# Turning the cached latents of one more sequence by on-chip transfers and VectorE instead of TensorE

## The reference

```
q_lat  = einsum('bqhd,chd->bqhc', q_nope, w_uk)            # 8 samples, 8 heads, 128 latents
s_past = einsum('bqhc,bkc->bhqk', q_lat, lat_past) + einsum('bqhr,bkr->bhqk', q_rope, kr_past)
p      = softmax(concat(s_past, s_new) * MLA_SCALE)
ctx    = einsum('bhqk,bkc->bqhc', p_past, lat_past) + p_new * c_kv
```

## Time and profile before

| | us |
|---|---|
| median of 3 runs | 1266.18 |
| lowest, highest | 1266.0, 1266.7 |
| the profiled execution | 1266.02 |
| its span, first to last instruction | 1264.2 |
| TensorE busy in it | 1250.9 (99%) |
| VectorE busy | 549.7 (43%) |
| ScalarE busy | 250.5 (20%) |

### The profile page before, as it was taken

One profiled execution on the slowest core, in us unless ns is written; L12 is line 12 of the kernel. 1 busy time (PEld: TensorE's weight loads), 2 busy tenths in 40 slices (PEclk: granted clock), 3 DMA queues, 4 the chain that ended last, 5 costly groups with the idle time before them and its releaser, 6 DMA issues.

```text
span 1264.2 us, 18049 instructions
## 1 busy us (share of the span) xinstructions
PE 1250.9 (99%) x7142; PEld 1022.8 (81%) x7142; DVE 549.7 (43%) x1387; ACT 250.5 (20%) x640; POOL 153.0 (12%) x210
## 2 busy tenths in 40 slices
PE   8999999999999999999999999999999999999997
PEld 6878777776888888888888787777778888888886
DVE  7866646323235333321178746463241453324212
ACT  3432414311100111110033324243111011111000
POOL 2012442010000000020001134511000000000000
PEclk9999999999999999999999999999999999999999
DMA  9433576357454444464454344755564544444440
GB/s 342 155 100 101 134 254 227 130 188 170 122 152 148 147 143 147 148 225 150 148 154 142 100 115 150 249 205 177 140 173 126 149 143 149 150 150 150 151 138 35
DMA packets 93971, 198.49 MB, mean 157 GB/s; under 512 B 41680, under 2 KB 42736, under 8 KB 91072
## 3 DMA queue, kind: packets, MB, share of 16 engines
q1 hardware_dynamic: 84624, 156.15, 40.4%
q0 software_dynamic: 8768, 40.84, 9.4%
q10 hardware_dynamic: 496, 0.36, 0.1%
HBM read 183.86 MB, written 9.25 MB: 153 GB/s over the span
## 4 chain that ended last, share of the span: by engine, by line
PE 95%; DVE 4%; ACT 1%; issue 0%; DMA 0%; SPq 0%; DVEq 0%; ACTq 0%
PE banks L573 77%; PE banks L1063 2%; PE banks L1076 1%; PE banks L1111 1%; PE banks L1074 1%; PE banks L968 1%; PE banks L717 1%; DVE arena L1715 1%; PE banks L996 1%; PE banks L675 0%; PE banks L1012 0%; DMA arena<-in_x 0%; DVE arena L2114 0%; PE banks L873 0%; PE banks L590 0%
## 5 line engine op out<-in xcount | busy, mean ns | idle before, releaser
L573 PE MATMUL banks<-arena 128*128 128x264 f32 x4512 | 1032.3, 388 | 5.7 <-DVE arena L1609 4.9
L573 PEld LDWEIGHTS banks<-arena 128*128 128x128 f32 x4512 | 851.0, 190 | 169.2 <-issue 13.2
L1217 ACT ACTIVATE arena<-banks 128x256 f32<-128x256 f32 (+8 forms) x252 | 92.6, 391 | 403.7 <-PE banks L573 293.2
L2217 DVE TENSOR_SCALAR arena<-arena 128x256 f32<-128x256 f32 x44 | 18.2, 414 | 130.2 <-ACT arena L1217 130.0
L2250 DVE SCALAR_TENSOR_TENSOR arena<-banks,arena 128x264 f32<-128x264 f32 x16 | 6.9, 433 | 134.2 <-PE banks L573 134.2
L2431 POOL COPY arena<-arena 128x2 f32<-128x2 f32 x44 | 13.7, 310 | 377.6 <-ACT arena L1217 275.9
L1248 ACT ACTIVATE arena<-banks 128x264 f32<-128x264 f32 x32 | 12.6, 392 | 130.6 <-PE banks L573 130.6
L2110 DVE COPY arena<-banks 128x512 f32<-128x512 f32 x24 | 16.6, 690 | 36.7 <-PE banks L1063 36.5
L1529 ACT ACTIVATE arena<-arena 128x256 f32<-128x256 f32 x44 | 18.4, 417 | 66.3 <-DVE arena L2219 66.3
L2224 DVE SCALAR_TENSOR_TENSOR arena<-arena 128x256 f32<-128x256 f32 x44 | 18.7, 426 | 26.6 <-ACT arena L1529 26.6
L2229 DVE TENSOR_TENSOR arena<-arena,banks 128x256 f32<-128x256 f32 x42 | 17.7, 422 | 26.4 <-PE banks L573 26.3
(11 more groups left out here) (447 smaller groups left out, 1072.5 us busy)
## 6 DMA issues: line engine op xcount, KB each, us to landing
arena<-in_weights SPq DMA_DIRECT2D x229, 512.0 KB, 3.6
arena<-in_weights SPq DMA_DIRECT2D x113, 256.0 KB, 3.5
arena<-in_s POOLq DMA_DIRECT2D x2, 2048.0 KB, 10.9
out_ss_o<-arena POOLq DMA_DIRECT2D x16, 256.0 KB, 3.1
arena<-in_mla_w POOLq DMA_DIRECT2D x4, 1024.0 KB, 6.7
arena<-arena SPq DMA_DIRECT2D x64, 64.0 KB, 2.4
arena<-in_c POOLq DMA_DIRECT2D x4, 512.0 KB, 6.3
out_sc_o<-arena POOLq DMA_DIRECT2D x16, 128.0 KB, 3.8
```

The costliest lines, as they stand in the source:

```text
L573: mm = nc.tensor.matmul(dst, ring[:, at_:at_ + 128], rhs[:, j, :], start=(start and j == 0), stop=(stop and j == k - 1))
L1217: return A(dst, src, ACT.Copy, scale=scale)
L2217: link(ts(cv, fc[:, j % 3, 0:TP], w[0], par[:, Q_FB + j:Q_FB + j + 1], ALU.mult, ALU.add))
```

## The change

Sequence 5 joins 6 and 7. Its blocks are laid out by 16 on-chip transfers, whose source is `lat[5]` and whose target is `ltt[:, 1]` itself, once the scores of sequence 3, the last reader of that half of `ltt`, are done. VectorE then turns them in place in `ltt[:, 1]`. TensorE no longer transposes sequence 5, and ScalarE and VectorE no longer copy its four banks. SyncE has the transfers ahead of unit 54 (sequence 5), 56 and 57 (sequences 6 and 7 as before).

VectorE's order: `turn(5)` comes right behind `pages(4)`, ahead of the three pieces that stood around `pages(5)`. The four pieces between sequences 5 and 6 become five, on all engines.

```diff
+IN_BLOCKS = 5, 6, 7
@@ schedule()
+    def mark(*sequences):
+        at_ = (34 + piece[0]) // 2 + SLOTS - 1
+        for n in sequences:
+            while at_ in marks:
+                at_ += 1
+            marks[at_] = n
     for n in range(4):
         pages(n)
+    mark(5)
     add("ss"); half(1); add("mxT", 1, "V"); ...
-    pages(4); half(2); pages(5); half(4); pages(6); pages(7); add("ss", 1, "A", 1)
+    pages(4); half(2); pages(5); half(5); pages(6); pages(7); add("ss", 1, "A", 1)
@@ build()
+        def blocks(n):
+            return lat[n - 6] if n >= 6 else ltt[:, n % 2].rearrange("p i n -> p (i n)")
@@ SyncE, blocks_of_latents
-                sp.wait_ge(*out(l, "cx", 0))
+                ...
+                elif n == 5:
+                    sp.wait_ge(*out(l, "ss", 0))
+                else:
+                    sp.wait_ge(*out(l, "cx", 0))
                 sp.wait_ge(*at(l, f"lat_in{n}", 32))
@@ TensorE, pages
-                    if n < 6:
+                    if n not in IN_BLOCKS:
                         for i in range(4):
                             b = claim("ltr", 4 * n + i)
...
-                        pe.wait_ge(*at(l, "lat_turned", 4 * (n - 5)))
+                        pe.wait_ge(*at(l, "lat_turned", 4 * (IN_BLOCKS.index(n) + 1)))
@@ TensorE
                 pages(5)
-                half(4)
+                half(5)
                 pages(6)
@@ ScalarE
                 pages(5)
-                half(6)
+                half(7)
@@ VectorE
+                def turn(n):
+                    dve.wait_ge(*at(l, f"lat_in{n}", 32))
+                    if n >= 2:
+                        dve.wait_ge(*scored(n - 2))
+                    V.transpose(krt[:, n % 2, :], key[n]).then_inc(*up("key_turned"))
+                    dve.wait_ge(*at(l, f"lat_blocks{n}", 256))
+                    for i in range(4):
+                        V.transpose(ltt[:, n % 2, i, :], blocks(n)[:, 512 * i:512 * i + 512]).then_inc(*up("lat_turned"))
                 pages(4)
-                half(2)
-                pages(5)
-                half(4)
-                pages(6)
-                pages(7)
+                turn(5)
+                half(3)
+                half(5)
+                turn(6)
+                half(1)
+                turn(7)
+                half(1)
                 top(1, 2)
```

More of the change, by code:

```diff
@@ L98, in schedule @@
 def schedule():
-    s, piece = [], [0]
+    s, piece, marks = [], [0], {}
+    def mark(*sequences):
[4 more added lines that the diff above has]
+            marks[at_] = n
     def add(name, n=1, reader="A", first=0):
@@ L149, in schedule @@
         pages(n)
+    mark(5)
     add("ss"); half(1); add("mxT", 1, "V"); half(1); add("mxB", 1, "V"); half(3); add("lsum", 1, "V"); add("cx")
-    at_context = (34 + piece[0]) // 2
+    mark(6, 7)
     half(2); add("cmb", 1, "V")
-    pages(4); half(2); pages(5); half(4); pages(6); pages(7); add("ss", 1, "A", 1)
+    pages(4); half(2); pages(5); half(5); pages(6); pages(7); add("ss", 1, "A", 1)
     half(2); add("mxT", 1, "V", 1); half(1); add("mxB", 1, "V", 1); half(4); add("lsum", 1, "V", 1); add("cx", 1, "A", 1); half(3); add("cmb", 1, "V", 1); half(len(PIECES) - piece[0])
@@ L160, in schedule @@
     add("fd", 8, "V")
-    return s, at_context + SLOTS - 1
+    return s, marks
 SCHED, BLOCKS_AT = schedule()
@@ L201 @@
     decay_masked=1, diag_set=3, ffn_conv=22, ffn_sconv=2, ffn_stanh=2, ffn_tail=22, ffn_tanh=22, ffn_zeros=1, fh_loaded=16,
-    hidden=2, hidden_norm=16, norm_raw=16, norm_square=16, norm_sum=14, hist_loaded=16, key_copied=2, key_turned=8, lat_turned=8, **{f"lat_blocks{n}": 256 for n in (6, 7)}, **{f"lat_in{n}": 32 for n in range(8)},
+    hidden=2, hidden_norm=16, norm_raw=16, norm_square=16, norm_sum=14, hist_loaded=16, key_copied=2, key_turned=8, lat_turned=12, **{f"lat_blocks{n}": 256 for n in IN_BLOCKS}, **{f"lat_in{n}": 32 for n in range(8)},
     inverse=1, inverse_turned=1, m_loaded=64, mdecay_exp=1, mdecay_in=4, mdecay_masked=1, merged=8, mla_q=16, mla_kv=16,
@@ L458, in build @@
         last_rms = bank("fd", 1)[:, 0:TT]
+        def blocks(n):
+            return lat[n - 6] if n >= 6 else ltt[:, n % 2].rearrange("p i n -> p (i n)")
         def quarter_of_latents(n, b, q):
-            return (lat[n - 6][32 * q:32 * q + 32, 512 * b:512 * b + 512].rearrange("i (r j) -> i r j", r=NR),
+            return (blocks(n)[32 * q:32 * q + 32, 512 * b:512 * b + 512].rearrange("i (r j) -> i r j", r=NR),
                     lat[n][32 * b:32 * b + 32, :].rearrange("i (r q j) -> i r q j", r=NR, q=4)[:, :, q, :])
@@ L499, in blocks_of_latents @@
             def blocks_of_latents(l, n):
-                sp.wait_ge(*out(l, "cx", 0))
+                if n == 0:
+                    sp.wait_ge(*out(l, "uq", 7))
+                elif n == 4:
+                    sp.wait_ge(*at(l, "page_scored", 3))
+                elif n == 5:
+                    sp.wait_ge(*out(l, "ss", 0))
+                else:
+                    sp.wait_ge(*out(l, "cx", 0))
                 sp.wait_ge(*at(l, f"lat_in{n}", 32))
@@ L512, in _ @@
                     sp.wait_ge(w_started, u - SLOTS + 2)
-                if u % UNITS in (BLOCKS_AT, BLOCKS_AT + 1):
-                    blocks_of_latents(u // UNITS, 6 + u % UNITS - BLOCKS_AT)
+                if u % UNITS in BLOCKS_AT:
+                    blocks_of_latents(u // UNITS, BLOCKS_AT[u % UNITS])
                 for h, at_, n in runs[u]:
@@ L1070, in pages @@
                     else:
-                        pe.wait_ge(*at(l, "lat_turned", 4 * (n - 5)))
+                        pe.wait_ge(*at(l, "lat_turned", 4 * (IN_BLOCKS.index(n) + 1)))
                     for i in range(4):
-                        turned = heads(ltt[:, n % 2, i, :], 32) if n >= 6 else turned_lat(n)[:, :, 32 * i:32 * i + 32]
+                        turned = heads(ltt[:, n % 2, i, :], 32) if n in IN_BLOCKS else turned_lat(n)[:, :, 32 * i:32 * i + 32]
                         nc.tensor.matmul(heads(sb[32 * i:32 * i + 32, :], 32), ql_pad[:, g, s_, :], turned,
@@ L1471, in pages @@
                 def pages(n):
-                    for i in (0, 2):
+                    for i in () if n in IN_BLOCKS else (0, 2):
                         act.wait_ge(*out(l, "ltr", 4 * n + i))
@@ L2050, in _, with scored @@
                 last.then_inc(*up("query_blocks"))
+                def scored(n):
+                    if n % 4 == 3:
+                        return out(l, "ss", n // 4)
+                    return at(l, "page_scored", 3 * (n // 4) + n % 4 + 1)
+                def turn(n):
[6 more added lines that the diff above has]
+                        V.transpose(ltt[:, n % 2, i, :], blocks(n)[:, 512 * i:512 * i + 512]).then_inc(*up("lat_turned"))
                 def masked(g):
@@ L2094, in _ @@
                 dve.wait_ge(*at(l, "st_conv", 16))
[L2096 to L2100, removed]
                 def pages(n):
@@ L2106, in pages @@
                     V.transpose(krt[:, n % 2, :], key[n]).then_inc(*up("key_turned"))
[L2107 to L2114, removed]
+                    for i in (1, 3):
+                        dve.wait_ge(*out(l, "ltr", 4 * n + i))
+                        V.tensor_copy(ltt[:, n % 2, i, :], bank("ltr", 4 * n + i)).then_inc(*read("ltr", 4 * n + i))
                     half(1)
```

## The result

The changed kernel takes 1269.7 us (median of 19 runs) against 1266.26 us before (20 runs): a ratio of 1.0024, 95% interval 1.0017 to 1.0030. It is slower by 3.4 us, a quarter of a per cent, and the forecast of 1266.8 us, with a range up to 1268.6, is missed.

The account below looks back on a forecast made before the run. TensorE, busy 99% of the span, was taken as the bound. Per layer -1.73 - 0.23 + 2.28 gave +0.31, two layers +0.6 on 1266.02: 1266.6 profiled, 1266.8 us as median, range 1265.4 to 1268.6.

Parts of the forecast that it names:

- The transposes removed: TensorE, ahead of the scores of sequence 5: without its 16 transposes these come 1.73 us earlier per layer.
- The turning of 5 free: VectorE turns sequence 5 by 289.0, TensorE asks at 294.30: no wait, 5.3 us to spare, cost nothing.
- The moved piece: Piece 75 now precedes VectorE's turning of sequence 6, so TensorE waits 2.28 us per layer before the scores of 6.
- the wait at 7: TensorE's existing wait for VectorE before the scores of sequence 7, 0.23 us by the starts, was to go.
- The sum of +0.3 per layer: Scores of sequence 7 and the same work end 0.31 us later per layer: -1.73 - 0.23 + 2.28, less rounding.
- SyncE's room: SyncE's queue takes 16 more transfers in its pause before 278.93; blocks of 6 up to 0.8 us later, cost nothing.
- The clock falls in the wait: Rival: TensorE's clock halves in the wait before the scores of 6, +3.8 us per layer, 1274.5 in all; chance 0.04.

Follow-up runs that it names:

- the kernel shifted by eight matmuls: The changed kernel with eight unread TensorE matmuls per layer where sequence 5's transposes stood, so the wait comes 3.57 us later: 1277.21 us, ratio 1.0082.

## Why the prediction was wrong, step by step

- **The transposes removed, -1.73 us:** right. The run of three pieces takes 5.43 us (294.47 - 289.04; forecast 5.45).
- **The turning of 5 free:** right. It is done at 289.06, TensorE asks at 294.47.
- **The moved piece, a new wait of 2.28 us:** right. By the starts it is 309.49 - 296.43 - 10.79 = 2.27, and the wait at 7 is gone. The sum of +0.3 per layer holds: the scores of 7 end 26.24 us after the three pieces start (315.28 - 289.04), forecast 26.28. The experiments give each term by itself, for two layers: -3.4 us for the turning alone, +3.9 for the moved piece alone, +0.55 for both with the wait filled.
- **SyncE's room:** the size was wrong, with no effect on this kernel. I allowed the blocks of 6 a delay of 0.8 us ("279.1 at the most" should have been 279.8 by the rows: 266.02 + 11.55 + 2.20); they started 2.8 us later (281.75 against 278.93), since the first sixteen transfers took 12.1 us and the four loads behind them 3.3 us instead of 1.6 to 2.2. The wait at 6 hid it. With four pieces the delay reached TensorE, by half a microsecond in layer 0 of the profile.
- **"The clock falls in the wait", chance 0.04:** this is the step that failed. The sum had no term for the clock, and the rival that named it, the right mechanism, had far too small a chance. By their times the clock fell in 28 of 29 runs of the changed kernel, in one layer or both, for about 1.7 us each. What stood against it, that TensorE is busy for all but 2.3 us around the wait, is so, but no row showed that this keeps the clock up. The clock of 1.00 across a wait of 0.15 us said nothing of one fifteen times as long. The price was too high: 3.8 us per layer was forecast, for a clock down from the first score to the end of piece 77; it fell 1.0 us later and rose within the piece, which cost 1.70.

The trace of before held better evidence than was used. I took from the kernel's end only its mean clock, 0.52. With TensorE's last matmuls and the stretch ahead of it, it also says when the clock fell:

```profile
1258.32 0.38 PE L1183 MATMUL banks<-arena 32*128 32x8 f32 x2
```

```profile
1258.00:1260.00 2.00, 0.71 (x6) 0.49 (x4) 1.26 (x4) 0.00 (x0) 0.00 (x0) 1.00 0.00 0
```

TensorE ends at 1258.70. The clock is 1.00 up to 1260.00, and a mean of 0.52 over the next 4.2 us, with 0.50 as the lower level, leaves about 0.2 us at the upper one. So it fell about 1.5 us after the last matmul, within less idle time than the 2.28 us that the forecast put into each layer (there were two short gaps ahead of it, of 0.43 and 0.47 us). The kernel's start is the other long idle stretch, 4.95 us. There the view reads 1.00, but the first four matmuls of line 573 take twice as long as four of them later:

```profile
4.95 2.13 PE L573 MATMUL banks<-arena 128*128 128x264 f32 x4 [4.95 <-DVE arena L1609]
```

```profile
13.06 1.05 PE L573 MATMUL banks<-arena 128*128 128x264 f32 x4
```

That is the pace of the lower level; whether the clock or late operands set it, the trace does not settle.

The forecast time was thus that of runs without a fall: 1266.45, a single run, and 1266.75 with the wait filled. The range had to reach to 1266.8 + 3.5. The Trainium skill (TensorE: Matmul & The Clock Gate, "Part 1: The HAM clock gate (the "warmup" mystery)") says that the throttled state is the default, released by activity. The runs agree: filling the wait with work keeps the clock up in 11 of 11 runs.

What stays open is why the share of runs with a fall changes with the shift, and why runs of one kernel differ; the traces show which clock is granted, not what decides it.

## What to carry to other kernels

- A wait of TensorE, where it bounds the kernel, can have two prices: its length, and what a fall of its clock costs behind it. Here the second was paid in most runs with 2.2 us of idle time and in none with 1.67. Look at the clocks and times of all runs, not at one profile.
- When a piece of cover is moved, follow it on every engine that reads it out. The changed kernel costs 3.4 us or brings 4.1, by whether VectorE turns sequence 6 behind or ahead of one read-out.

## What the runs showed that I had not expected

- Two waits of 1.67 us left the clock up in 11 of 11 runs; of 2.20 us they brought it down in 28 of 29 at one place, and in 3 of 9 with two more matmuls ahead, 0.89 us later; at 2.80 us each run had a fall, mostly in one of the two layers.
- A fall of the clock need not come within the wait. In the changed kernel it came 1.0 us after TensorE had resumed; with 2.80 us of wait, and with 2.21 us in the kernel shifted by eight matmuls, the first score matmuls were already slow (1.87 and 1.72 us instead of 1.00).
- Sixteen on-chip transfers of 64 KB hold SyncE's queue for 10.7 to 12.8 us in the changed kernel's profile. The four loads behind the first of them took 3.30 us in layer 0 and 2.04 us in layer 1, against a usual 1.6 to 2.2.
